# DeltaNet scan: the two levels of the triangular inverses as 32x32 products on diagonal pieces of TensorE's array

## The reference

```python
def gated_delta_chunked(q, k, v, beta, g, s0):   # chunks of 64 tokens
    ...
    lmat = jnp.where(strict, jnp.einsum('bhnik,bhnjk->bhnij', k_beta, k) * decay, 0.0)
    tmat = lax.linalg.triangular_solve(eye + lmat, eye, left_side=True, lower=True, unit_diagonal=True)
    u = jnp.einsum('bhnij,bhnjv->bhniv', tmat, v_beta)
    ...
    def step(S, xs):
        v_new = u_c - jnp.einsum('bhck,bhkv->bhcv', w_c, S)
        o_c = jnp.einsum('bhck,bhkv->bhcv', q_c, S) + jnp.einsum('bhij,bhjv->bhiv', a_c, v_new)
        S = S * jnp.exp(gl_c)[..., None, None] + jnp.einsum('bhck,bhcv->bhkv', k_c, v_new)
```

## Time and profile before

| what | value |
|---|---|
| median of three runs | 2447.23 us |
| profiled execution | 2445.34 us, its span 2443.4 us |
| mean granted TensorE clock | 0.936 |
| PE / DVE / ACT / POOL busy | 2140.3 / 923.2 / 673.7 / 224.6 us |
| L901, the 64x64 products: x5120 from SBUF tiles alone | 172.1 us busy, 222 ns mean of one, 36.2 us idle before |
| L1688, the masks: x40 | 27.7 us busy, 692 ns each, 54.0 us idle before |

### The profile page before, as it was taken

The page is one execution under the profiler, slowest core; times in us unless marked ns, Lnnn a source line. Parts: engine busy times, 40 slices in busy tenths (PEclk is TensorE's granted clock), DMA queues, the critical chain, the costliest instruction groups (busy, mean ns, idle before and its releaser), DMA issues. The chain is left out here.

```text
span 2443.4 us, 39149 instructions
## 1 busy us (share of the span) xinstructions
PE 2140.3 (88%) x16431; PEld 1315.9 (54%) x16431; DVE 923.2 (38%) x1700; ACT 673.7 (28%) x1366; POOL 224.6 (9%) x301
## 2 busy tenths in 40 slices
PE   5986999998999499998979999999998698899960
PEld 4555566774554388887635555554455444444420
DVE  3154666653775367666550010101233210001126
ACT  6131766652442133331320000000111122122223
POOL 2000100000000233332000000000000000000013
PEclk8997999999999599999999999999998799999985
DMA  9323100001000233333111111120314365775225
GB/s 330 130 103 96 31 4 2 1 2 60 26 13 0 38 53 63 68 65 57 36 62 43 42 26 26 26 69 2 146 69 148 119 211 189 254 241 189 94 98 205
DMA packets 256381, 210.08 MB, mean 86 GB/s; under 512 B 147468, under 2 KB 219472, under 8 KB 255568
## 3 DMA queue, kind: packets, MB, share of 16 engines
q1 hardware_dynamic: 242032, 158.16, 22.0%
q0 software_dynamic: 9136, 31.06, 3.9%
q10 hardware_dynamic: 5040, 18.35, 1.8%
HBM read 165.37 MB, written 42.01 MB: 85 GB/s over the span
## 5 line engine op out<-in xcount | busy, mean ns | idle before, releaser
L742 PE MATMUL ps<-R 128*128 128x512 f32 (+1 forms) x816 | 301.4, 530 | 11.0 <-SPq L530 8.4
L1009 PE MATMUL ps<-R 128*128 128x512 f32 (+1 forms) x768 | 285.9, 526 | 19.5 <-DMA R<-in_w_dn_br_dram 17.4
L1085 PE MATMUL ps<-R 128*128 x560 | 256.4, 612 | 24.4 <-SPq L654 21.2
L742 PEld LDWEIGHTS ps<-R 128*128 128x128 f32 x816 | 158.7, 195 | 150.7 <-issue 132.6
L1009 PEld LDWEIGHTS ps<-R 128*128 128x128 f32 x768 | 147.1, 192 | 151.8 <-issue 144.5
L901 PE MATMUL ps<-R 64*64 64x64 f32 x5120 | 172.1, 222 | 36.2 <-DVE R L1688 25.2
L1085 PEld LDWEIGHTS ps<-R 128*128 128x128 f32 x560 | 109.3, 197 | 166.0 <-issue 166.0
L901 PEld LDWEIGHTS ps<-R 64*64 64x64 f32 x5120 | 161.4, 137 | 54.1 <-DVE R L1688 28.4
L1763 DVE TENSOR_TENSOR R<-ps,R 128x512 f32<-128x512 f32 (+1 forms) x48 | 28.9, 603 | 393.6 <-ACT R L1342 392.8
L1930 DVE COPY R<-ps 128x256 f32<-128x256 f32 x35 | 14.9, 425 | 378.1 <-PE ps L1110 378.1
L1524 DVE TENSOR_SCALAR_CACHE_REDUCE R<-ps 128x512 f32<-128x512 f32 (+1 forms) x208 | 128.4, 666 | 59.9 <-PE ps L827 59.8
(11 more groups left out here) (270 smaller groups left out, 2657.8 us busy)
## 6 DMA issues: line engine op xcount, KB each, us to landing
R<-in_w_mod_dram SPq DMA_DIRECT2D x12, 2048.0 KB, 9.1
slot_output<-R ACTq DMA_DIRECT2D x35, 512.0 KB, 3.5
R<-in_w_gate_e_dram SPq DMA_DIRECT2D x16, 1024.0 KB, 7.4
R<-in_w_up_e_dram SPq DMA_DIRECT2D x16, 1024.0 KB, 10.3
R<-in_w_down_e_dram SPq DMA_DIRECT2D x16, 1024.0 KB, 12.3
R<-in_w_in_dram SPq DMA_DIRECT2D x30, 512.0 KB, 5.5
R<-tu_scratch SPq DMA_DIRECT2D x80, 128.0 KB, 3.2
R<-in_x_sample_dram SPq DMA_DIRECT2D x16, 512.0 KB, 5.7
```

What stands on the lines that cost most here:

```text
L742: last = mm(ps[:, u % 4, 0:w], w_sb[n % NW][:, k, :], hT[:, k, c0:c0 + w], start=(k == 0), stop=(k == KD - 1))
L1009: mm(ps[:, o + x, 0:w], wk[:, x, k, :], hT[:, k, c0:c0 + w], start=(k == 0), stop=(k == KD - 1))
L1085: last = mm(ps[:, 2 + t % 2, :], hsT[t % 2][:, k, :], R[:, bass.ds(at + (RB + k * 512), 512)], start=(k == 0), stop=(k == KD - 1))
```

## The change

The products of both levels work on 32x32 pieces only. At level 4 the result is wanted only inside the 32x32 blocks on the diagonal, so `blocks32` multiplies those, on the four diagonal pieces of the array in turn: 32 matmuls (64 instructions in the trace) in place of 16 (32). At level 5 only one 32x32 corner of each 64x64 matrix is wanted, and 16 matmuls of that size compute it (32 instructions, as before). The corners of `u5` now go to bank 2 and not to bank 3. Since the rest of banks 3 and 4 is no longer written, and DVE still subtracts whole banks, banks 2 to 4 are set to zero once before the scan (`past_in` counts it). The upper mask becomes a copy of the corners; the last subtraction becomes two `scalar_tensor_tensor` instructions, one per direction, with a factor of -1 or 0 per partition (`minus_half`), so `u5_ready` counts two per step.

```diff
+            def blocks32(bank, lhs, rhs):
+                for a in range(PAIRS):
+                    for lo in range(0, P, 32):
+                        cols = slice(lo % C, lo % C + 32)
+                        last = mm(ps[lo:lo + 32, bank, a * C + lo % C:a * C + lo % C + 32], lhs(a)[lo:lo + 32, cols], rhs(a)[lo:lo + 32, cols], start=True, stop=True)
...
+                        pe.wait_ge(S["u5_ready"], 2 * s)
-                    product(2, lt, t_).then_inc(S["x4_mm"], 1)
+                    blocks32(2, lt, t_).then_inc(S["x4_mm"], 1)
...
-                    product(3, u_, x_).then_inc(S["t4_mm"], 1)
+                    blocks32(3, u_, x_).then_inc(S["t4_mm"], 1)
...
-                    product(4, x_, u_).then_inc(S["u4_mm"], 1)
+                    blocks32(4, x_, u_).then_inc(S["u4_mm"], 1)
...
-                    product(2, lt, t_).then_inc(S["x5_mm"], 1)
+                    for a, (rows, lines) in enumerate(CORNER):        # CORNER = [(0, 32)] * 4 + [(32, 0)] * 4
+                        for h in (0, C):
+                            last = mm(ps[h + lines:h + lines + 32, 2, a * C + rows:a * C + rows + 32], lt(a)[h + rows:h + rows + 32, lines:lines + 32],
+                                      t_(a)[h + rows:h + rows + 32, rows:rows + 32], start=True, stop=True)
...
-                    product(3, x_, u_).then_inc(S["u5_mm"], 1)
+                    for a, (rows, lines) in enumerate(CORNER):
+                        for h in (0, C):
+                            last = mm(ps[h + rows:h + rows + 32, 2, a * C + lines:a * C + lines + 32], x_(a)[h + lines:h + lines + 32, rows:rows + 32],
+                                      u_(a)[h + lines:h + lines + 32, lines:lines + 32], start=True, stop=True)
...
+            v.memset(ps[:, 2:5, :], 0.0).then_inc(S["past_in"], 1)
...
-                    masked(xm, 2, 1)
+                    v.tensor_copy(at(xm, 0, (4 * C + 32, 2), (C, 4), (1, 32)), at(bank8(2), 0, (4 * C + 32, 2), (C, 4), (1, 32))).then_inc(S["x5_ready"], 1)
...
-                    v.tensor_tensor(u_, u_, bank8(3), ALU.subtract).then_inc(S["u5_ready"], 1)
+                    for d in range(2):
+                        cols = slice(32 - 32 * d, C - 32 * d)
+                        u_d = u_[:, 4 * d:4 * d + 4, cols]
+                        v.scalar_tensor_tensor(u_d, bank8(2)[:, 4 * d:4 * d + 4, cols], minus_half[:, d:d + 1], u_d, ALU.mult, ALU.add).then_inc(S["u5_ready"], 1)
```

More of the change, by code:

```diff
@@ L68, in shape_constants @@
     before = (part[:, None] < free[None, :]).astype(np.float32)
-    parts = [np.eye(P), same, np.ones((P, P))] + upto + after_bd + level + [eye, -eye, rot, before, (part[:, None] // 16) % 2 == np.arange(2)[None, :]]
+    parts = [np.eye(P), same, np.ones((P, P))] + upto + after_bd + level + [eye, -eye, rot, before, (part[:, None] // 16) % 2 == np.arange(2)[None, :],
+            -1.0 * ((part[:, None] // 32) % 2 == np.arange(2)[None, :])]
     return np.concatenate([np.asarray(a, np.float32) for a in parts], axis=1)
@@ L129, in build @@
         levels = take(2 * 2 * C).rearrange("p (l d c) -> p l d c", l=2, d=2)
-        eye_st, neg_eye, rot, before, block_dir = take(C), take(C), take(P), take(P), take(2)
+        eye_st, neg_eye, rot, before, block_dir, minus_half = take(C), take(C), take(P), take(P), take(2), take(2)
         small = sb("small", [P, small_np.shape[1]])
@@ L317, in build @@
         LAST = (C - 1, 0)
+        CORNER = [(0, 32)] * 4 + [(32, 0)] * 4
         oF = R1[:, 0:4 * T].rearrange("p (a t) -> p a t", a=4)
@@ L894, in _ @@
             pe.wait_ge(S["arrivals"], 5 * 3)
-            pe.wait_ge(S["past_in"], 96 + 64 + 1)
+            pe.wait_ge(S["past_in"], 96 + 64 + 2)
             halves = [slice(0, C), slice(C, 2 * C)]
@@ L901, in product @@
                         last = mm(ps[lo, bank, a * C:(a + 1) * C], lhs(a)[lo], rhs(a)[lo], start=start and (alone or a == 0), stop=stop and (alone or a == PAIRS - 1))
+                return last
+            def blocks32(bank, lhs, rhs):
[3 more added lines that the diff above has]
+                        last = mm(ps[lo:lo + 32, bank, a * C + lo % C:a * C + lo % C + 32], lhs(a)[lo:lo + 32, cols], rhs(a)[lo:lo + 32, cols], start=True, stop=True)
                 return last
@@ L934, in _ @@
                     if s > 0:
-                        pe.wait_ge(S["u5_ready"], s)
-                    product(3, u_, x_).then_inc(S["t4_mm"], 1)
+                        pe.wait_ge(S["u5_ready"], 2 * s)
+                    blocks32(3, u_, x_).then_inc(S["t4_mm"], 1)
                     if s > 0:
                         pe.wait_ge(S["u4_ready"], s)
-                    product(4, x_, u_).then_inc(S["u4_mm"], 1)
+                    blocks32(4, x_, u_).then_inc(S["u4_mm"], 1)
                     product(5, feature(s, 1), lambda a: eye_st).then_inc(S["kt_mm"], 1)
@@ L944, in _ @@
                     pe.wait_ge(S["t4_ready"], s + 1)
-                    product(2, lt, t_).then_inc(S["x5_mm"], 1)
+                    for a, (rows, lines) in enumerate(CORNER):
+                        for h in (0, C):
+                            last = mm(ps[h + lines:h + lines + 32, 2, a * C + rows:a * C + rows + 32], lt(a)[h + rows:h + rows + 32, lines:lines + 32],
+                                      t_(a)[h + rows:h + rows + 32, rows:rows + 32], start=True, stop=True)
+                    last.then_inc(S["x5_mm"], 1)
                     pe.wait_ge(S["kd_ready"], 2 * (s + 1))
@@ L959, in _ @@
                     pe.wait_ge(S["u4_ready"], s + 1)
-                    product(3, x_, u_).then_inc(S["u5_mm"], 1)
+                    for a, (rows, lines) in enumerate(CORNER):
+                        for h in (0, C):
+                            last = mm(ps[h + rows:h + rows + 32, 2, a * C + lines:a * C + lines + 32], x_(a)[h + lines:h + lines + 32, rows:rows + 32],
+                                      u_(a)[h + lines:h + lines + 32, lines:lines + 32], start=True, stop=True)
+                    last.then_inc(S["u5_mm"], 1)
                     pe.wait_ge(S["qd_ready"], 2 * (s + 1))
@@ L964, in _ @@
                     product(7, lambda a: state(s)[:, a, :], lambda a: qd[:, a, :], stop=False, alone=False).then_inc(S["qs_mm"], 1)
-                    pe.wait_ge(S["u5_ready"], s + 1)
+                    pe.wait_ge(S["u5_ready"], 2 * (s + 1))
                     pe.wait_ge(S["r_ready"], s + 1)
@@ L1645, in _ @@
             dve.wait_ge(S["dve_chain"], count("dve_chain"))
-            dve.wait_ge(S["past_in"], 96 + 64 + 1)
+            v.memset(ps[:, 2:5, :], 0.0).then_inc(S["past_in"], 1)
+            dve.wait_ge(S["past_in"], 96 + 64 + 2)
             def at(x, o, *dims):
```

## The result

The change made the kernel slower: 2460.93 us (median of six runs, 2455.72 to 2463.12) against 2447.85 (six runs), a ratio of 1.0049 [1.0031, 1.0068], so +12 us (the two medians are 13 apart). The forecast was 2438.5, with 2423 to 2453 as range: the time lies outside it, on the other side.

What follows compares the result with a forecast made beforehand. SP's transfer chain and PE's product chain tie at 18.8 us per pair, then share a mostly DVE segment. Terms -2.5 - 3.3 - 0.8 - 2.3 + 0.4 = -8.5 us gave 2438.5, range 2423 to 2453.

Steps and rivals of the forecast that it cites:

- The rate of the wide product: Level 4's x4, t4, u4, 64 instructions on four pieces: 0.6 us each taken, saving 0.33 us each.
- the corner product: Level 5's x5 and u5, 32 instructions on two pieces: 0.5 us each taken, saving 0.43 us each.
- the change of size: PE switching between tile sizes: 0.09 us charged each, eight more in the stream, 0.75 us.
- the copy and the pair of L1758: On DVE: corner copy 425 ns in place of 692; two L1758 instructions together about the 0.69 us of before.
- the fill: Zeroing three banks once before the scan: 1.6 us, hidden behind POOL's work but for 0.4 with the signal.
- The subtraction of `u5`: DVE's last step in the common segment: starts at about 1.55 us, 1.94 after the mask before; -0.4 us per pair.
- PE's chain falls to 17 us, and SP's stays at 18.8: Per pair of steps: PE's products up to DVE's next blocks shorten, so SP's transfer round trip bounds; -2.5 us in all.
- the last pair: The last two steps have no blocks or decays, so PE bounds behind x4: 1.1 us saved per step, -2.3.
- The saving that goes through: Rival, chance 0.12: SP has slack, so each pair shortens by PE's whole saving, 2.15 us; time 2425.
- a piece that needs 58 ns whatever the columns: Rival, chance 0.13: narrower is not shorter, all five products stay at 0.93 us; 2453, or 2450 with SP's slack.
- The slower one: Rival, chance 0.13: instructions cost 26 to 29 ns on four pieces too, wide products take 1.7 us; +47, some 2493.
- The idle time before `u5`: PE's 1.06 us wait grows by 1.75 and more per pair, lowering its clock; -0.37 per pair, -3.3 us over nine.

Runs made afterwards that it cites:

- level 5 alone: The change with level 4 back to whole 64x64 products and no fill of banks, against the kernel before: ratio 0.9974, -6 us.
- half of the pieces: The change with level 4 on pieces 0 and 64 alone, 32 instructions per product, half of its blocks left out; against before: 0.9971, -7 us.
- level 5 with x4: The change with t4 and u4 back to 64x64 products, x4 still on four pieces, against the kernel before: ratio 0.9956, -11 us.
- the bursts: The kernel before plus three matmul bursts behind the scan (32x32 on four pieces, 32x32 on two, 64x64 on two), no semaphores inside: one run, 2524.1 us.

## Why the prediction was wrong

*The rate of the wide product* was right: 97 instructions in 1.03 us, less one's 0.19, are 8.8 ns each, 0.56 us for 64 (0.6 taken). So were the corner product (0.60 - 0.19 = 0.41 for 31 intervals, 0.42, where 0.5 was taken), the change of size (the last L957 starts at 1019.90 + 0.41 = 1020.31, the next at 1020.43), the copy and the pair of L1758, and the fill (1.34 us for 1.6; PE waited 11.20 us there for 10.67, 0.5 more where 0.4 was taken). The subtraction of `u5` starts 1.47 us after the copy, 1.55 forecast:

```profile
1006.19 0.42 DVE L1744 COPY R<-ps 128x256 f32<-128x256 f32 x1
1006.53 1.21 DVE L1751 TENSOR_TENSOR R<-ps,R 128x1024 f32<-128x1024 f32 x1
1007.66 0.60 DVE L1758 SCALAR_TENSOR_TENSOR R<-ps,cst,R 128x128 f32<-128x128 f32 x2
```

*The step that failed* is "PE's chain falls to 17 us, and SP's stays at 18.8. So SP's is late next". It was summed from the times of single products and took for granted that the instructions are there. They were not, and PE's chain is 20.7 us long in the pair shown, not 17. The supply of the program, a cost that the sum has at nothing, took 33.7 us in 26 stalls. The stalls, about one per step, put PE's chain back in front, and behind the last pair, where PE bounds alone, they fall due in full: 0.86, 1.08 and 2.41 us in two steps where -2.3 was forecast.

```profile
1173.94 0.32 PE L957 MATMUL ps<-R 32*32 32x32 f32 x9 [0.86 <-issue]
```

*The rivals.* The saving that goes through and a piece that needs 58 ns whatever the columns can be told from the rows: in the kernels nearly without stalls no more than 11 us were gained, where the first would have given 22 for the whole change, and a piece took 4 x 8.8 = 35 ns per instruction on four pieces and 26 on two. The slower one was about the right resource with the wrong law. It had a price per instruction, 26 to 29 ns, and would have given +47. What is limited is the supply over 256 instructions: 3.5 us at the least, 27 ns per matmul with its weights on average, while a shorter run goes at 8.8 ns. The rows before could hardly show it: nowhere in that kernel did PE take less than 3.73 us for 128 matmul instructions with their weights, just above that, and no stall stands in it. In the change a quarter of all such stretches of the scan are under 3.4 us, the quickest 1.24. I took the 26 to 29 ns of two stretches for the columns' doing, rightly, and did not ask whether a long stretch had ever gone faster; there was none.

*The rest of the sum.* The forecast's -8.5 us is near what kernels nearly without stalls gave, level 5 alone -6, half of the pieces -7, level 5 with x4 -11; but none of them is the whole change, and one way to the number was not as forecast. The idle time before `u5` was to grow by the 1.75 us and more in each pair. It was 18.2 us in nine cases before and 18.6 with level 5 alone; with half of the pieces, which has all small products, it was 24.3, so 0.7 us in each. The lower clock in the scan did come: 0.94 in the change, and 0.95 with half of the pieces, nearly without stalls. The part that gives SP's chain the pair is half supported. With half of the pieces DVE waited for the landing in eight of ten cases, 18.4 us in all, the forecast's "nearly every pair" and "15 us and more"; with level 5 alone it was 12.3 us in five. And a shorter chain of SP's gave 5, 6 and 3 us on three kernels, whatever PE's chain was.

## What to carry to other kernels

Count instructions per time on TensorE and not just columns: where 256 instructions in a row (weights count too, and a float32 matmul is four) take less than about 3.5 us, PE will run dry, and the profile calls it "issue" with no semaphore. Cutting a product into more, smaller ones cost 11 us where two such products follow each other and did no harm where slow instructions surround it; cutting it to a corner with the same number of instructions paid here. When two chains tie, order the queue of the one that holds no compute: moving four DMA issues into a landing time gave 5 us on the kernel before, for nothing.

## What was not expected of the hardware

- The supply of the program was 3.47 to 3.75 us per 256 instructions in a quiet stretch; where stalls in the scan lie one piece apart, PE went on 3.5 to 4.1 us after it had gone on the last time. In the bursts the next piece was fetched only once PE had entered the one before it.
- In the scan most stalls lie 1024 instructions, four pieces, apart. One step is 518 matmul instructions, with their weights 1036, so the one stretch per step that is too fast, `t4` and `u4`, comes round every four pieces. The length of a stall is what the piece before leaves of the round trip (median 3.8 us over the 26 stalls, PE's own work in it 1.2 to 3.2). Whether other transfers delay the supply was not tried.
- The pieces of the program can be counted in the list of DMA queues: 47 packets of the instruction queue in the stretch of the earlier trace rows before, 56 after. PE's instructions there, with their weights, are 47 and 55 times 256.

```profile
q8 instruction: 56, 0.92, 1.6%
```

- Four diagonal 32x32 pieces took 8.8 ns per float32 matmul instruction, two took 13.2, against 29 for 64x64 on two. So at the full clock four are 1.5 times as fast as two, not twice. In the bursts at half clock 128 instructions took 1.93 us on four and 3.62 on two, which is close to twice.
